# Second layer's output product, norms and the first recurrent input slabs in two halves of 512 tokens; its narrow slabs in two pieces of 512

## The reference

```python
y = jnp.concatenate([y_conv, y_ret, y_na], axis=-1) @ w_out      # 1024 x 1024
x_new = layer_norm(DEEPNORM_ALPHA * x + gate[:, None] * y, ln_g, ln_b)
...
h = rms_norm(x, g_mix_pre[l])
z = h @ w_in[l]                     # u_rx, u_rg: 1024 columns each
...
xc = causal_dwconv(xb, conv_w, conv_b)          # 4 taps
gates = jnp.einsum('bshi,ghij->gbshj', xh, w_gates)
r = jax.nn.sigmoid(gates[0]); i = jax.nn.sigmoid(gates[1])
log_a = -LRU_C * r * jax.nn.softplus(-lru_lambda)
a = jnp.exp(log_a); mult = jnp.sqrt(-jnp.expm1(2.0 * log_a))
u = mult * i * xc                   # then h_t = a_t h_(t-1) + u_t
return h * jax.nn.gelu(gb)
```

## Time and profile before

| | |
|---|---|
| median of 3 runs | 3222.71 us (3217.47 to 3224.88) |
| span of the profiled execution | 3217.7 us |
| TensorE busy | 3113.9 us, 97% |
| VectorE busy | 1520.9 us, 47% |
| ScalarE busy | 730.5 us, 23% |
| POOL busy | 1130.2 us, 35% |
| weight loads by SP | 225 of 512 KB |

### The profile page before, as it was taken

The page is one execution under the profiler, slowest core; times in us unless marked ns, Lnnn a source line. Parts: engine busy times, 40 slices in busy tenths (PEclk is TensorE's granted clock), DMA queues, the critical chain, the costliest instruction groups (busy, mean ns, idle before and its releaser), DMA issues.

```text
span 3217.7 us, 41353 instructions
## 1 busy us (share of the span) xinstructions
PE 3113.9 (97%) x17368; PEld 2525.2 (78%) x17368; DVE 1520.9 (47%) x1657; ACT 730.5 (23%) x943; POOL 1130.2 (35%) x525
## 2 busy tenths in 40 slices
PE   6999998999999999899999999999899999999998
PEld 5877876788878787798577788788688888888877
DVE  3134418428643424823676601443664155155477
ACT  2011215312231123510345411112211001101132
POOL 2232220126643232044133444353244344443442
PEclk9999999999999999999999999999999999999999
DMA  6200111333231011112111111112211111111211
GB/s 245 72 33 8 35 41 48 111 127 121 72 129 33 14 41 46 54 40 102 68 53 40 46 46 50 40 53 101 83 46 46 52 46 52 46 46 52 106 45 72
DMA packets 60189, 206.07 MB, mean 64 GB/s; under 512 B 5905, under 2 KB 7697, under 8 KB 60049
## 3 DMA queue, kind: packets, MB, share of 16 engines
q1 hardware_dynamic: 42240, 142.62, 13.7%
q10 hardware_dynamic: 17808, 61.39, 5.1%
HBM read 187.22 MB, written 16.78 MB: 63 GB/s over the span
## 4 chain that ended last, share of the span: by engine, by line
PE 77%; DVE 9%; issue 8%; POOL 3%; DMA 2%; ACT 1%; POOLq 0%; SPq 0%; DVEq 0%; ACTq 0%
PE ps L575 66%; DVE Sb L1908 3%; DMA raw<-s 2%; PE ps L886 2%; POOL w_hi L494 2%; POOL w_lo L496 1%; DVE C L2139 1%; PE ps L1074 1%; PE ps L796 1%; PE ps L711 1%; PE ps L550 1%; PE ps L603 1%; PE ps L1055 0%; PE ps L802 0%; DVE g_lo L2220 0%
## 5 line engine op out<-in xcount | busy, mean ns | idle before, releaser
L494 POOL TENSOR_TENSOR w_hi<-raw,pool_zero 128x1024 fp32r<-128x1024 f32 (+2 forms) x242 | 456.8, 1887 | 1993.1 <-PE ps L575 1788.3
L496 POOL TENSOR_TENSOR w_lo<-raw,w_hi 128x1024 fp32r<-128x1024 f32 (+2 forms) x242 | 638.6, 2639 | 19.0
L575 PE MATMUL ps<-h_hi,w_hi 128*128 128x512 f32 (+1 forms) x1760 | 469.5, 362 | 6.6 <-POOL w_lo L496 4.6
L575 PE MATMUL ps<-g_hi,w_hi 128*128 128x512 f32 x1488 | 465.6, 394 | 2.1 <-DVE g_lo L2220 1.5
L575 PE MATMUL ps<-g_lo,w_hi 128*128 128x512 f32 x1488 | 459.8, 390 | 0.0
L575 PE MATMUL ps<-g_hi,w_lo 128*128 128x512 f32 x1488 | 459.1, 390 | 0.0
L575 PE MATMUL ps<-h_hi,w_lo 128*128 128x512 f32 (+1 forms) x1760 | 449.6, 351 | 0.0
L575 PE MATMUL ps<-h_lo,w_hi 128*128 128x512 f32 (+1 forms) x1760 | 449.5, 351 | 0.0
L575 PEld LDWEIGHTS ps<-h_hi,w_hi 128*128 128x128 f32 x1760 | 288.4, 188 | 74.1 <-issue 26.4
L575 PEld LDWEIGHTS ps<-g_hi,w_hi 128*128 128x128 f32 x1488 | 278.9, 188 | 67.0 <-issue 7.0
L575 PEld LDWEIGHTS ps<-g_lo,w_hi 128*128 128x128 f32 x1488 | 280.3, 188 | 58.6
(11 more groups left out here) (341 smaller groups left out, 3591.9 us busy)
## 6 DMA issues: line engine op xcount, KB each, us to landing
raw<-s SPq DMA_DIRECT2D x225, 512.0 KB, 3.5
modring<-modw ACTq DMA_DIRECT2D x32, 512.0 KB, 4.5
x_saved<-Y ACTq DMA_DIRECT2D x2, 4096.0 KB, 12.8
modfirst<-modw SPq DMA_DIRECT2D x4, 1024.0 KB, 18.0
modfirst<-modw ACTq DMA_DIRECT2D x4, 1024.0 KB, 24.9
xin<-x_saved ACTq DMA_DIRECT2D x1, 4096.0 KB, 12.9
B<-x_saved ACTq DMA_DIRECT2D x1, 4096.0 KB, 15.1
x_saved<-B ACTq DMA_DIRECT2D x1, 4096.0 KB, 13.4
```

The lines of the kernel that those rows point to most:

```text
L494: G.tensor_tensor(w_hi[s][:, :n], raw[s][:, :n], zero.to_broadcast([P, n]), ALU.add).then_inc(hi_done, 1)
L496: G.tensor_tensor(w_lo[s][:, :n], raw[s][:, :n], w_hi[s][:, :n].bitcast(F32), ALU.subtract)\
L575: last = T.matmul(ps[:, o + c0:o + c0 + size], wt[s][:, kk], xx[:, k, t0:t0 + size], start=(x == 0 and n == 0), stop=(x == k_n - 1 and n = ...
```

## The change

- `XPART` goes; the 17 slabs of the second layer use `XONLY`: two matmuls of 512 columns for each weight tile, columns side by side in PSUM. The evacuations follow (`skip` goes).
- The second layer's output product becomes 16 slabs of 512 columns (tokens 0 to 511, then 512 to 1023), with the weights loaded and split twice. Its operands are written to `g_hi` and `g_lo` instead of `h_hi` and `h_lo`; the low part of chunk 0 is now made behind the last product of the convolution.
- Both norms run for each half: the sums over features by VectorE's additions, then matmuls against one column of ones (4 of 128x1), a root and a reciprocal of 128x4, and transposes that spread it over the partitions. Squares and the shift by `lnb1` are ScalarE's. TensorE's small matmuls stand inside the slabs, at places given by (slab, chunk). The residuals of the second half stand inside VectorE's passes of the first.
- The first six recurrent slabs (blocks 0 to 2) are split too: the first half of the tokens (`G_RHEAD`, six slabs) in front of the second half's norms, the second half behind them, with three buffers more for their results. That is 14 more slabs to load and split in all.
- The gate maps stand at other places. The loads of the gate maps' weights (`rgwt`) come earlier; the stream is stored in two halves.

```diff
-        XPART = [(CTX, CTX, 512 - CTX), (512, 512, 512), (1024, 1024, 256)]
...
-                part = FULL if l == 0 else XPART
+                part = FULL if l == 0 else XONLY
...
-                gemm(g0 + G_OUT, 8, h_hi, h_lo, segs, 3, SPLITS["y1"], order=Y_ORDER, between=last_tile)
-
-                keep_busy(6, 6)
...
+                def last_variance(h):
+
+                    pe.wait_ge(lx_add, 7 * (3 + h))
+                    last_columns(h, VARIANCE).then_inc(lx_var, 1)
...
+                half = [[(0, 0, 512)], [(512, 0, 512)]]
+                for n in range(KD):
+                    slab(g0 + G_OUT + n, n % 2, g_hi, g_lo, KD, half[0], 3, SPLITS["y1"] if n == 0 else None,
+                         between=y_idle if n == 0 else None, order=Y_ORDER if n == 0 else None)
+                for n in range(KD):
+                    slab(G_OUT_B + n, n % 2, g_hi, g_lo, KD, half[1], 3,
+                         between=at_points(n, 0, [(0, 3), (2, 5), (3, 2), (5, 7), (6, 4)]))
+                for c in range(R_HEAD):
+                    slab(G_RHEAD + c, c % 2, g_hi, g_lo, KD, half[0], 3, SPLITS["h2a"] if c == 0 else None,
+                         between=at_points(c, 1, [(0, 5), (2, 5), (3, 2), (5, 4), (5, 7)]))
...
-            first_pair(G_RNN, g_hi, g_lo, "h2", 0)
-            for c in range(1, 8):
-                slab(G_RNN + 2 * c, 0, g_hi, g_lo, KD, SEC, 2, between=rnn_gate_maps(c - 1))
-                slab(G_RNN + 2 * c + 1, 1, g_hi, g_lo, KD, SEC, 2)
+            first_pair(G_RNN, g_hi, g_lo, "h2b", 2, segs=(half[1], half[1]), dead=2, freed=G_RNN - 1)
+            for c in range(2, R_HEAD):
+                slab(G_RNN + c, c % 2, g_hi, g_lo, KD, half[1], 2, between=rnn_gate_maps(0, 4) if c == 3 else None)
+            gate_maps_in = {6: (1, 1), 7: (2, 5), 9: (3, 2), 10: (4, 6), 12: (5, 4), 14: (6, 4)}
+            for c in range(R_HEAD, 16):
+                slab(G_RNN + c, c % 2, g_hi, g_lo, KD, SEC, 2,
+                     between=rnn_gate_maps(*gate_maps_in[c]) if c in gate_maps_in else None)
```

ScalarE's order in the new part, and two of its helpers:

```diff
+                def shifted(h, k0, k1):
+
+                    full, cut = LAST[h]
+                    for k in range(k0, k1):
+                        act.wait_ge(lx_norm, 8 * (2 + h) + k + 1)
+                        if k >= 3:
+                            act.wait_ge(mx_add, 7 * h + k - 2)
+                        to = sq_last[k % 2] if k else sum_last
+                        A.activation(to[:, cut], Y[:, k, full], ACT.Square, bias=vcol("lnb1", k)).then_inc(mx_sq, 1)
+                        A.activation(Y[:, k, full], Y[:, k, full], ACT.Identity, bias=vcol("lnb1", k)).then_inc(mx_x, 1)
...
+                last_squares(0, 0, KD)
+                last_deviation(0)
+                shifted(0, 0, KD)
+                kept(0)
+                mix_deviation(0)
+                mix_highs(0)
+                last_squares(1, 0, 4)
+                head(0)
+                last_squares(1, 4, KD)
+                head(1)
+                last_deviation(1)
+                head(2)
+                shifted(1, 0, 4)
+                head(3)
+                shifted(1, 4, KD)
+                kept(1)
+                head(4)
+                mix_deviation(1)
+                head(5)
+                mix_highs(1)
```

VectorE's passes and their order (a dictionary gives the chunk after which a residual of the second half stands):

```diff
+                def normalised(h, behind):
+
+                    full, cut = LAST[h]
...
+                    dve.wait_ge(lx_spread, 3 + h)
+                    for k in range(KD):
+                        V.scalar_tensor_tensor(Y[:, k, full], Y[:, k, full], ln_gain[:, 1, k:k + 1],
+                                               ps[:, SPREAD * BANK:(SPREAD + 1) * BANK], ALU.mult, ALU.mult)\
+                            .then_inc(lx_norm, 1)
+                        if k >= 2:
+                            add_square(k - 1)
+                        if k in behind:
+                            residual(1, behind[k])
+                    add_square(KD - 1)
...
+                for n in range(KD):
+                    residual(0, n)
+                centred(0, {4: 0})
+                residual(1, 1)
+                inverse(0)
+                normalised(0, {1: 2, 5: 3})
+                residual(1, 4)
+                mix_inverse(0)
+                mixed(0, {0: 5, 4: 6})
+                residual(1, 7)
+                centred(1, {})
+                inverse(1)
+                normalised(1, {})
+                mix_inverse(1)
+                mixed(1, {})
```

More of the change, by code:

```diff
@@ L1020, in _, with last_mean, last_columns @@
                     continue
-                segs = XONLY
-                def last_tile(k):
+                def last_mean(h):
+                    pe.wait_ge(lx_sum, 3 + h)
+                    T.matmul(ps[:, MEANS * BANK:(MEANS + 1) * BANK], ones, sum_last[:, LAST[h][1]], start=True, stop=True)\
+                        .then_inc(lx_mean, 1)
+                def last_columns(h, bank):
+                    for t in range(4):
+                        c0 = LAST[h][1].start + t * P
+                        last = T.matmul(ps[:, bank * BANK + t:bank * BANK + t + 1], sum_last[:, c0:c0 + P], ones[:, 0:1],
+                                        start=True, stop=True, skip_group_check=True)
+                    return last
@@ L1026, in last_tile, with y_idle @@
+                def y_idle(k):
                     if k == 6:
                         keep_busy(6, 3)
-                gemm(g0 + G_OUT, 8, h_hi, h_lo, segs, 3, SPLITS["y1"], order=Y_ORDER, between=last_tile)
-                keep_busy(6, 6)
[L1032 to L1053, removed]
-                    for t0, c0, size in SEC:
-                        last = T.matmul(ps[:, 4 * BANK + c0:4 * BANK + c0 + size], ones, sq[:, t0:t0 + size],
-                                        start=(k == 0), stop=(k == KD - 1))
-                    last.then_inc(stat_used, 1)
@@ L1676, in _ @@
             ple(1)
[L1677 removed]
+            roots(3)
             ple(2)
@@ new lines, in mix_inverse, with mixed @@
+                def mix_inverse(h):
+                    dve.wait_ge(mx_std, h + 1)
+                    V.reciprocal(rc[:, 1, 4:8], rc[:, 0, 4:8]).then_inc(mx_inv, 1)
+                def mixed(h, behind):
+                    full, cut = LAST[h]
+                    name = ("h2a", "h2b")[h]
+                    dve.wait_ge(mx_x, 8 * (h + 1))
+                    dve.wait_ge(mx_spread, h + 1)
+                    for k in range(KD + 1):
+                        if k < KD:
+                            V.scalar_tensor_tensor(xin[:, k, full], Y[:, k, full], vcol("g_mix_pre", k),
+                                                   ps[:, FACTOR * BANK:(FACTOR + 1) * BANK], ALU.mult, ALU.mult)\
+                                .then_inc(sp_tmp, 1)
+                        if k:
+                            dve.wait_ge(sp_hi, SPLITS[name] + k)
+                            V.tensor_tensor(g_lo[:, k - 1, cut], xin[:, k - 1, full], g_hi[:, k - 1, cut].bitcast(F32),
+                                            ALU.subtract).then_inc(sp_lo, 1)
+                        if k in behind:
+                            residual(1, behind[k])
```

309 lines of the change are left out of this document (194 added, 115 removed).

## The result

The changed kernel takes 3241.87 us in the median (3237.83 to 3242.94, 4 runs), the kernel before beside it 3223.8. The ratio is 1.0059, with a 95% interval of 1.0045 to 1.0073: slower by 14 to 24 us. The forecast was 3228, with a range of 3200 to 3244. The time lies inside the range and on the side I gave the largest of three close chances (0.36), but the forecast of +5 is under a third of the measured 18, and the time lies above the main case's own range (3219 to 3237).

What follows compares the result with a forecast made beforehand. TensorE, busy 97% of the span, was taken as the bound, with 60.6 us of only means, sums of squares and fillers to hide. Terms -5.4 + 10.2 + 0.6 = +5.4 us took the median from 3222.7 to 3228, range 3200 to 3244.

Steps and rivals of the forecast that it cites:

- main case: Whole kernel: the summed terms give +5.4 us, median 3228, own range 3219 to 3237; chance 0.42.
- (a): After the last convolution slab: first half slab, waiting for y's last chunk, ends at +11.4 us instead of +5.5.
- (b): First product half: third slab waits for the first one's bank, which wants `xin`, and starts at +21 us.
- (c): First product half: six half slabs of 5.45 us and a little pacing bring the time to +54 us.
- (d): Second product half and six recurrent first halves: VectorE is longer than TensorE, 114 us, bounds 81 and 125.
- (e): Recurrent pair to first gate map: VectorE-paced slab, bare POOL split, another slab and the way to the map, 23.5 us.
- first to last map: Recurrent blocks: a ring over ScalarE and VectorE, lengthened by POOL's splits, sets the turns; 177.3 us, +0.6.
- the hand-overs in (d): Second product half and heads: two means at 1.2, four crossings at 4.4, 2 for the first low part: 22 us.
- the lock: Second product half and heads: VectorE's SBUF-to-SBUF operations stand still during POOL's; 2.4 us a split, 34 us over 14.
- cold clock: Rival: waits without fillers drop TensorE to 1.2 GHz, 5 us, half inside waits anyway, giving 3231; chance 0.12.
- Faster: Rival: POOL's hold on VectorE costs half, 1.2 us a split and 1.7 a recurrent turn, giving 3199; chance 0.28.
- Slower: Rival: before the pair, VectorE gets one addition per POOL operation, 2.8 us a step, +11 to +20, centre 3243; chance 0.18.

Runs made afterwards that it cites:

- experiment 1: The kernel before with only the second layer's 17 narrower slabs, two pieces of 512 columns: ratio 0.9983 to the kernel before, 3216.07 us.
- second trace: Trace of the unaltered changed kernel, measured a second time in a later run: ratio 1.0056 to the kernel before, 3237.86 us.
- experiment 4: The changed kernel with POOL splitting only 8 columns for the 16 recurrent slabs behind the second norm (different results): ratio 0.9975 to the kernel before, 3213.81 us.
- experiment 6: The changed kernel with short fillers in front of TensorE's waits, ten places: ratio 1.0034 to the kernel before, 3233.32 us.
- 3: The changed kernel with 8-column splits for the second product half and six recurrent first halves (different results): ratio 0.9971 to the kernel before, 3211.43 us.
- experiment 8: The changed kernel without recurrent heads: 16 recurrent slabs whole, product and norms still in halves, fillers behind the product: ratio 1.0014 to the kernel before, 3226.02 us.

## Why the prediction was right in direction and too small in size

The steps, as the prediction has them:

| step | forecast | measured |
|---|---|---|
| narrower slabs | -5.4 | -3.7 in the trace; -5.2 alone (experiment 1) |
| (a) first half slab ends | +11.4 | +13.1 |
| (b) third slab starts | +21 | +22.5 |
| (c) six half slabs | +54 | +58.2 |
| (d) other half and heads | 114 | 123.4 |
| (e) pair to first map | 23.5 | 28.2 |
| first to last map | 177.3 | 175.8 |
| whole, to the last map | +5.4 | +24.0 |

(a) to (c) count from the last convolution slab's end, 1449.6; the six half slabs end at 1507.8. The second trace of the changed kernel has 58.6 for (c), 119.5 for (d), 28.0 for (e) and 175.8 between the maps: a stretch such as (d) is known to some 4 us only.

**Right.** The places of the waits; that VectorE is the longer engine in (d); that the turns stay at 25 us and TensorE's 24 us of work done ahead aren't given back; that no reciprocal of 6.6 is left; the price of the narrower slabs. The reason given for the turns, a ring lengthened by splits, holds for the first four (4 shows it). The forecast had every map wait for the convolution; the last three don't, because TensorE has whole slabs again there and needs 72.9 us for them.

**The term of the sum that was mis-sized most is the hand-overs in (d)**, four crossings at 4.4, two means at 1.2 and 2 for the first low part, 22 in all. The 2 are work of VectorE, so 20 stand against its idle time there, which sums to 31 (28 in the second trace): in the four crossings it stood idle for 5.0, 6.9, 7.7 and 6.3, and for 5 in the two means and in small waits. Its work without the lock was 63.5 instead of 60, and the lock 29 instead of 34 (2.1 a split, not 2.4), so these two nearly cancel: 63.5+29+31=123.5. I had taken the crossing from the first layer's reciprocal, 1.45 after its last addition, and had counted too little for the second part, the spread: the reciprocal is done in 0.2 us, but TensorE reaches the place only five chunks behind the sum, 4.4 us warm and 6 to 7 us cold (three chunks in the last crossing, 5.7 us cold). The chunks could be counted in the diff. The first part was longer too: in the last three crossings VectorE waited 3.4, 2.4 and 2.5 us for the root, not 1.45.

**The second is the cold clock.** The rival gave it 3 us; experiment 6 took some 8 back, of which its trace shows 3.7 in the second half of (d). The slab behind the wait for `xin` took 8.3 us instead of 5.4, which is all that (c) lost behind (b). My argument that half of it lies inside waits left out that the small matmuls which VectorE waits for stand behind cold chunks. It shares time with the crossings (9), so the two can't be summed.

**The third is (e).** The pair's first slab ended after 12.4 us instead of 9.5, with one low part of 2.19 behind a split and a stretch at a granted clock of 0.83; slab 2 and the way to the map took 10.6 instead of 8.9, with its first matmuls cold behind the wait for the split. The split itself has the forecast length (5.0 for 4.9). Without POOL (e) is 21.7 (experiment 4), where slab 2 starts without a wait.

**The rivals.** *Faster* (the lock costs half) is refuted: 3 and 4 took out 28 and 27 us, where half the price would have given 12 to 17 in 3. *Slower* gave 3243 and set its point at (d) above 116; (d) passed it and the time came out at 3242, but its mechanism did not act as stated. A step costs 2.8 us only while POOL has a split, as from 1536.6 to 1549; beside an idle POOL it falls back to 1.3, and the lock came out under the main case's price. (That price rested on 3.3 us lost to one and a half splits in the earlier trace rows; the trace has the loss in the one whole split alone, since the half ran beside subtractions that read PSUM.) Its time was met for another reason. The upper end of the range, 3244, had been set for this rival, so it was luck that it held. *Cold clock* was true, and larger than priced.

**What stays open.** Of the 3.5 us of work above 60 in (d), 0.8 is the first half's last residual, which the count left out; the rest is not separated. Where (a) lost its 1.7 wasn't tried. The narrower slabs show 3.7 and 2.4 in the two traces of the changed kernel and 5.2 in the medians of experiment 1, whose interval is 2.6 to 8.7. Of the 8 us of experiment 6 the part ahead of the second mean (3.7) can't be told from the scatter between two traces.

## What to carry to other kernels

Work moved ahead of a stage pays only as far as the stage's next longest path allows. Here TensorE paced the recurrent turns (25.2 us each, never idle in experiment 8), so moving its work ahead looked worthwhile; but a ring over the other engines, with the splits in it, was as long, and it gave nothing back. Before a stage is split to fill an idle stretch, look for such a ring in the next one. Here the idle stretch was better made shorter (small roots and reciprocals, each half's crossing beside the other's pass) than filled: filling it brought 14 more splits, and each held up VectorE's operations from SBUF to SBUF, by some 2 us (29 over 14). When small matmuls are set inside slabs, count the chunks between the sum and the place where its inverse is spread, at the clock that the engine will have after a wait.

## What the runs showed of the hardware

Behind such waits TensorE issued a matmul of 512 columns every 0.427 us, elsewhere every 0.227 (their recorded lengths are 0.63 and 0.39): the two levels 1.2 and 2.4 GHz.

```profile
1531.01 0.63 PE L584 MATMUL ps<-g_hi,w_hi 128*128 128x512 f32 x1
...
1540.16 0.39 PE L584 MATMUL ps<-g_hi,w_lo 128*128 128x512 f32 x1
```

The Trainium skill (TensorE: Matmul & The Clock Gate, "Part 1: The HAM clock gate") says that an idle array falls to the lower clock and must be busy again to leave it; the windows of experiment 6, at 1.00 where the changed kernel had 0.81 and 0.68, agree. New to me was that even behind a wait of 2.4 us (the first variance, 1527.08) the matmuls turned cold, at 1529.3, after starting warm, and that part of the cost came by way of VectorE, which waited for small matmuls queued behind the cold ones.

The lock is seen from both sides, and who starts first decides. In the trace above POOL's `w_hi` was 0.02 us ahead of the addition at 1537.25: `w_hi` took 1.89 and the addition 2.42. In the second trace the same addition was 0.01 us ahead (1538.83 and 1538.84): it took 0.68, and `w_hi` 2.43. The two traces differ by 3.9 us in (d), 3.3 of them between the two means; whether this order is the reason is not shown. In the recurrent blocks two taps of the first convolution took 6.08 us in the changed kernel, and 2.60 in experiment 4, without splits.
